# Turning the residual unscaled during the second block's output product, and one factor per token for two norms

## The reference, cut to what matters

```python
# end of the first block (layer B)
    x = x + (merged * jax.nn.silu(gate)) @ w_out_b[i]          # product "out_b"
return rmsnorm(x, norm_f)                                      # first norm
# start of the second block
shift, scale, gate = jnp.split(ada_mod(c, ada_w[i], ada_b[i]), 3, axis=-1)
h = rms_norm(x, norm_g[i]) * (1.0 + scale) + shift             # second norm, modulation
u, v, z = jnp.split(h @ w_in, 3, axis=-1)                      # products "in_v", "in_uz"
...
x = x + gate * out                                             # needs the normed x again

def rmsnorm(x, g):
    inv = lax.rsqrt(jnp.mean(xf * xf, axis=-1, keepdims=True) + RMS_EPS)
    return (xf * inv).astype(x.dtype) * g
```

## Time and profile before

| what | value |
|---|---|
| median of 3 runs | 2236.38 us (2232.61 to 2237.01) |
| profiled execution, first to last instruction | 2226.7 us |
| profiled execution's own time | not recorded apart from its span |
| TensorE busy | 2117.5 us, 95% |
| VectorE busy | 1566.4 us, 70% |
| ScalarE busy | 1079.3 us, 48% |
| HBM read | 518.00 MB, 235 GB/s over the span |

### The profile page before, as it was taken

One profiled execution on the slowest core, in us unless ns is written; L12 is line 12 of the kernel. 1 busy time (PEld: TensorE's weight loads), 2 busy tenths in 40 slices (PEclk: granted clock), 3 DMA queues, 4 the chain that ended last, 5 costly groups with the idle time before them and its releaser, 6 DMA issues. The chain is left out here.

```text
span 2226.7 us, 29663 instructions
## 1 busy us (share of the span) xinstructions
PE 2117.5 (95%) x9730; PEld 1750.1 (79%) x9730; DVE 1566.4 (70%) x2498; ACT 1079.3 (48%) x1644; POOL 11.1 (0%) x24
## 2 busy tenths in 40 slices
PE   6999999998999999979699999999999979999988
PEld 5888788887887878757588888888888868778866
DVE  5676777776789797866677777777866565556654
ACT  5444455444354445433544444544444365867732
POOL 0000000000000000000000000000000000000000
PEclk9999999999999999989799999999999989999999
DMA  6776678777766656646377878777755536434333
GB/s 275 282 287 240 235 271 321 277 289 250 275 255 238 235 226 246 230 179 254 143 287 279 306 290 296 285 283 296 281 211 177 189 133 226 173 131 148 135 132 132
DMA packets 92449, 523.32 MB, mean 235 GB/s; under 512 B 10288, under 2 KB 10416, under 8 KB 46288
## 3 DMA queue, kind: packets, MB, share of 16 engines
q1 hardware_dynamic: 89936, 510.64, 62.1%
q0 software_dynamic: 1888, 7.41, 0.9%
q10 hardware_dynamic: 544, 4.19, 0.5%
HBM read 518.00 MB, written 4.19 MB: 235 GB/s over the span
## 5 line engine op out<-in xcount | busy, mean ns | idle before, releaser
L807 ACT ACTIVATE w_hi<-raw 128x1024 fp32r<-128x1024 f32 (+1 forms) x704 | 722.1, 1046 | 946.2 <-PE bank L413 527.1
L1318 DVE TENSOR_TENSOR w_lo<-raw,w_hi 128x1024 fp32r<-128x1024 f32 (+1 forms) x704 | 829.2, 1206 | 220.1 <-ACT w_hi L807 219.5
L413 PE MATMUL bank<-w_hi,xa_hi 128*128 128x512 f32 x1952 | 773.9, 396 | 8.6 <-issue 6.1
L413 PE MATMUL bank<-w_hi,xa_lo 128*128 128x512 f32 x1952 | 764.6, 392 | 0.0
L413 PE MATMUL bank<-w_lo,xa_hi 128*128 128x512 f32 x1952 | 764.5, 392 | 0.0
L413 PEld LDWEIGHTS bank<-w_hi,xa_hi 128*128 128x128 f32 x1952 | 369.5, 189 | 86.2 <-issue 8.6
L413 PEld LDWEIGHTS bank<-w_hi,xa_lo 128*128 128x128 f32 x1952 | 369.2, 189 | 78.6
L413 PEld LDWEIGHTS bank<-w_lo,xa_hi 128*128 128x128 f32 x1952 | 369.3, 189 | 74.8
L413 PE MATMUL bank<-w_hi,xb_hi 128*128 128x512 f32 (+2 forms) x864 | 336.2, 389 | 8.5 <-DVE rbuf L1455 3.6
L413 PE MATMUL bank<-w_hi,xb_lo 128*128 128x512 f32 (+2 forms) x864 | 329.5, 381 | 0.0
L413 PE MATMUL bank<-w_lo,xb_hi 128*128 128x512 f32 (+2 forms) x864 | 329.4, 381 | 0.0
(11 more groups left out here) (204 smaller groups left out, 1204.2 us busy)
## 6 DMA issues: line engine op xcount, KB each, us to landing
raw<-units SPq DMA_DIRECT2D x352, 1024.0 KB, 4.8
ada_raw<-ada_units SPq DMA_DIRECT2D x258, 512.0 KB, 5.6
rows<-ln_rows POOLq DMA_DIRECT2D x8, 512.0 KB, 4.8
res<-x SPq DMA_DIRECT2D x2, 1024.0 KB, 6.5
held<-res ACTq DMA_DIRECT2D x1, 2048.0 KB, 8.6
res<-held ACTq DMA_DIRECT2D x1, 2048.0 KB, 7.9
out<-res SPq DMA_DIRECT2D x4, 512.0 KB, 7.4
silu_row<-c_row POOLq DMA_DIRECT2D x1, 1024.0 KB, 9.1
```

What stands on the lines that cost most here:

```text
L413: last = pe.matmul(ps[t][:, 0:cols], l, r, start=c == 0 and k == 0, stop=c == CPU * units_of - 1 and k == 2)
L807: act.activation(half_of(w_hi, n0, i), half_of(raw, n0, i), ACT.Copy).then_inc(hi_done, 1)
L1318: dve.tensor_tensor(half_of(w_lo, n0, i), half_of(raw, n0, i), half_of(w_hi, n0, i), ALU.subtract)\
```

## The change

The residual is no longer scaled before it is turned.

* During `out_b` blocks 2 and 3, TensorE turns the raw sums `res` of the finished blocks (`turn_sum`, six groups after a unit each, two more after the product). ScalarE copies each turned group to `side`, scaled per channel by `mul[:, 0]`, which is now norm_f * norm_g0 * (1 + scale0) (`scaled_group`).
* The sum of squares is taken by blocks: VectorE multiplies a block of `res` by a row of sqrt(norm_f^2 + eps) (`weigh_block`), ScalarE squares and sums it (`square_weighted`), and sums the plain squares (`square_plain`), which the first norm alone needs.
* At the border only block 3 is left to weigh and square. The reciprocal root is put on a diagonal, TensorE spreads it over the partitions with one product by ones (128x256), and VectorE multiplies each turned group by it (`scale_group`). ScalarE adds the shift and rounds to `xa_hi`, VectorE makes `xa_lo` (`lo_group`).
* The plain normed `res`, which the second block's residual sum needs, is made later: block 3's plain squares after the eighth group, and two pieces of `res` after every second block of `in_v`. The row norm_f is loaded a second time for it, from the GpSimd queue, because the first copy was overwritten by its root during `in_b`.
* Row sets that moved: `TURNS`, `SMALLS`, `HI0` and semaphore counts follow.

```diff
+            def turn_sum(g):
+
+                b0 = BLOCK0["out_b"] + g // 2
+                pe.wait_ge(bank_free[b0 % 2], read_out(b0))
+                turn(TURN0["xg"] + g, tiles(res, 2 * P * g))
+
+            product("out_b", 2, xb, then=turn_sum)
+            product("out_b", 3, xb, then=lambda q: turn_sum(4 + q) if q < 2 else None)
+            for g in (6, 7):
+                turn_sum(g)
+
+            pe.wait_ge(factor_ready, 1)
+            pe.matmul(use(SMALL0["xg"])[:, 0:S], ones, small[:, 0:S], start=True, stop=True).then_inc(small_done, 1)
...
+                if q in (7, 8, 12):
+                    b = {7: 0, 8: 1, 12: 2}[q]
+                    for t in range(NT):
+                        square_weighted(b, t, block_sums[:, t, b:b + 1])
+                    square_plain(b)
+                if 8 <= q < 14:
+                    scaled_group(q - 8)
...
-            b0 = BLOCK0["out_b"] + 3
-            residual_rms(bank_free[(b0 - 1) % 2], read_out(b0 - 1), bank_free[b0 % 2], read_out(b0))
-            residual_rms(res_normed, 3, res_normed, 4)
...
+            for t in range(NT):
+                square_weighted(3, t, stat[:, 68 + t:69 + t])
+                act.wait_ge(squared, 2 * 3 + t + 1)
+                last = act.activation(stat[:, 2 + t:3 + t], stat[:, 68 + t:69 + t], ACT.Sqrt, scale=1.0 / D,
+                                      bias=stat[:, 66 + t:67 + t])
+            last.then_inc(rms_ready, 1)
+            for g in (6, 7):
+                scaled_group(g)
+
+            for g in range(8):
+                act.wait_ge(scaled, g + 1)
...
+                last.then_inc(hi_turned, 1)
+                if g in (3, 5):
+                    split_hi(UNIT0["in_v"] + 2 + (g - 3) // 2)
+            act.wait_ge(rows_split, 8)
+            square_plain(3)
...
-            for j in range(4):
-                for t in range(NT):
-                    at = slice(j * NB, (j + 1) * NB)
-                    last = dve.scalar_tensor_tensor(out=res[:, t, at], in0=res[:, t, at], scalar=stat[:, 4 + t:5 + t],
-                                                    in1=rows[:, at], op0=ALU.mult, op1=ALU.mult)
-                last.then_inc(res_normed, 1)
...
-            residual_rows(4)
+            for t in range(NT):
+                last = dve.tensor_scalar(small[:, t * P:(t + 1) * P], ident, stat[:, 4 + t:5 + t], None, ALU.mult)
+            last.then_inc(factor_ready, 1)
...
+            dve.wait_ge(small_done, kf + 1)
+            for g in range(2):
+                scale_group(g)
+            for g in range(8):
+                lo_group(g)
+                if g < 6:
+                    scale_group(g + 2)
+                if g in (3, 5):
+                    n = (g - 3) // 2
+                    split_lo(UNIT0["in_v"] + 2 + n)
+                    add_ada(8 * ADA0["in_v"] + 2 + n)
...
             def in_v(j, first):
+                if first:
+                    dve.wait_ge(rms_ready, 4)
+                    steps.did(dve.reciprocal(stat[:, 84:86], stat[:, 82:84]))
+                    steps.wait()
+                    dve.wait_ge(row_in, 32)
...
+                for t in range(NT):
+                    cols = at_(res[:, t, :], NB * j, NB)
+                    last = dve.scalar_tensor_tensor(out=cols, in0=cols, scalar=stat[:, 84 + t:85 + t], in1=at_(rows, NB * j, NB),
+                                                    op0=ALU.mult, op1=ALU.mult)
```

More of the change, by code:

```diff
@@ L623, in in_v @@
                     product("in_v", i, xa, bs=2, us=8, j=j, first_group=TURN0["xg"] if now else None,
-                            ahead=(TURN0["xg"], side) if now else None, split=lambda g: g + 1)
+                            split=lambda g: g + 1)
             peeled(pe, 4, in_v)
@@ new lines, in scaled_group @@
+            def scaled_group(g):
+                act.wait_ge(turned, TURN0["xg"] + g + 1)
+                bank = turn_bank[(TURN0["xg"] + g) % 2]
+                for cc in range(2):
+                    c = 2 * g + cc
+                    last = act.activation(side_flat[:, c * S:(c + 1) * S], bank[:, cc * S:(cc + 1) * S], ACT.Copy,
+                                          scale=mul[:, 0, c:c + 1])
+                last.then_inc(turn_free[(TURN0["xg"] + g) % 2], 1)
+            act.wait_ge(gain_ready, 1)
@@ L1075, in modulated @@
+            act.wait_ge(rows_split, 8)
+            square_plain(3)
+            for t in range(NT):
+                steps.did(act.activation(plain_sums[:, t, :], plain_sums[:, t, :], ACT.Copy, accum_out=stat[:, 80 + t:81 + t]))
+            steps.wait()
+            act.activation(stat[:, 82:84], stat[:, 80:82], ACT.Sqrt, scale=1.0 / D, bias=eps).then_inc(rms_ready, 1)
             def modulated(g0, g, k, shift, n):
@@ L1473, in _ @@
                 dve.memset(stat[:, 72 + i:73 + i], 0.0).then_inc(s, 1)
+            steps.did(dve.memset(stat[:, 86:87], EPS * EPS))
+            steps.wait()
             residual_rows(1)
@@ L1682, in add_block, with gain, weigh_block @@
                     dve.tensor_tensor(dst, dst, banks[2 * (b0 % 2) + t][:], ALU.add).then_inc(bank_free[b0 % 2], 1)
+            def gain(k, name, scale):
+                return dve.scalar_tensor_tensor(out=mul[:, k, :], in0=mod[:, MOD0[scale]:MOD0[scale] + KC], scalar=1.0,
+                                                in1=v(name, 0, KC), op0=ALU.add, op1=ALU.mult)
+            def weigh_block(b):
+                b0 = BLOCK0["out_b"] + b
+                dve.wait_ge(root_row, 2)
+                for t in range(NT):
+                    dve.wait_ge(bank_free[b0 % 2], read_out(b0) - 1 + t)
+                    if b:
+                        dve.wait_ge(squared, 2 * b - 1 + t)
+                    dve.tensor_tensor(rbuf[:, t, :], res[:, t, b * NB:(b + 1) * NB], rows[:, b * NB:(b + 1) * NB], ALU.mult)\
+                        .then_inc(weighted, 1)
             n0, m0 = UNIT0["out_b"], 8 * ADA0["out_b"] + 2
             for q in range(16):
+                if q == 2:
+                    dve.wait_ge(mod_ready, MOD0["gate0"] // 4)
+                    steps.did(gain(0, "norm_g0", "scale0"))
+                    steps.wait()
+                    dve.tensor_tensor(mul[:, 0, :], mul[:, 0, :], v("norm_f", 0, KC), ALU.mult).then_inc(gain_ready, 1)
                 if q < 6:
@@ L1716, in _ @@
                     add_block("out_b", b)
+                    weigh_block(b)
                 if q == 13:
@@ new lines, in scale_group, with lo_group @@
+            def scale_group(g):
+                tg = TURN0["xg"] + g
+                dve.wait_ge(turn_free[tg % 2], tg // 2 + 2)
+                if g >= 4:
+                    dve.wait_ge(rows_split, g - 3)
+                dve.tensor_tensor(row_group(g).rearrange("p (k s) -> p k s", k=2),
+                                  side_flat[:, 2 * g * S:2 * (g + 1) * S].rearrange("p (k s) -> p k s", k=2),
+                                  factor, ALU.mult).then_inc(scaled, 1)
+            def lo_group(g):
+                dve.wait_ge(hi_turned, HI0["xg"] + g + 1)
+                for cc in range(2):
+                    c = 2 * g + cc
+                    last = dve.scalar_tensor_tensor(out=chunk(xa, 1, c), in0=row_group(g)[:, cc * S:(cc + 1) * S],
+                                                    scalar=mod[:, MOD0["shift0"] + c:MOD0["shift0"] + c + 1],
+                                                    in1=chunk(xa, 0, c), op0=ALU.add, op1=ALU.subtract)
+                    if g == 7 and cc == 0:
+                        last.then_inc(small_free[kf % 2], 1)
+                last.then_inc(rows_split, 1)
```

96 lines of the change are left out of this document (59 added, 37 removed).

## The result

| what | before | after |
|---|---|---|
| median of 6 runs each, same chip | 2234.96 us (2232.39 to 2237.01) | 2227.11 us (2221.49 to 2228.31) |
| ratio, 95% interval | | 0.9969 (0.9954 to 0.9984) |
| the profiled execution's span | 2226.7 us | 2226.1 us, own time 2228.05 |
| TensorE busy in it | 2117.5 us | 2122.8 us |
| end of `out_b` to start of `in_v` | 22.45 us | 10.89 us |

The change gained 7.8 us of 2235; the interval allows 3.6 to 10.3. Yet the two profiled spans differ by 0.6 us only. Both facts are true, and the experiments were needed to see why.

A forecast was written before the change was run, and what follows sets the result against it. TensorE, busy 95% of the span, was taken as the bound, with the weights' supply about as fast. Terms -11.7, +2.6 and -0.9 give -10.0; with +3.0, -7.0 us: 2229.4 us, range 2224.4 to 2234.0.

The forecast's parts named there:

- The border, 22.45 to 10.8: Between the end of `out_b` and the start of `in_v`: 22.45 us shrinks to 10.8, -11.7 us.
- the step behind it: At the border, after the product by ones: first group scaled, `xa_hi` and `xa_lo` made, `in_v` able to start at 1066.75.
- Six turns, +2.6: Six groups turned inside `out_b`, where TensorE has no idle time, cost 0.44 us each, +2.6 us.
- ScalarE as the bound of `out_b`: Rival: twelve squares and six copies in `out_b`; if none were hidden, the whole is +7.9 us, 2244.3; chance 0.06.
- Block 0, -0.9: First block of `in_v`, up to unit 4: 25.97 us becomes 25.1, -0.9 us.
- the low clock: At the start of `in_v`, TensorE at half speed for 4.3 us, costing 2.0 us, open from 0 to 3.3.
- group 6: In block 0 of `in_v`: TensorE wants this group at 1085.1, `lo_group` ends it at 1085.5, 0.4 us late.
- the wait at unit 4: In `in_v` after block 0: the unit's first half is ready 0.95 us after TensorE wants it.
- Supply in `in_v`, +3.0: Rest of `in_v`: smaller lead and VectorE's 1.35 us after every second block delay the weights, +3.0 us, between 0 and 6.9.
- 9.7 above the span, which the change doesn't touch.: Whole kernel: the median 2236.38 us lies 9.7 above the profiled span of 2226.7, and this difference stays.
- That the supply keeps up whole (-8.5 to -11): Rival: in `in_v` weights keep pace and the border's gain arrives whole, -8.5 to -11 us, about 2226.4; chance 0.24.
- That the supply eats up everything: Rival: weights set the pace in `in_v` and `in_uz`, leaving about -1 us, 2235.3, within 0.2%; chance 0.20.

The follow-up runs named there:

- c_after: The changed kernel, unchanged, timed and profiled once more against the kernel before: 2225.33 us, ratio 0.9966.
- c_before: The kernel before, unchanged, timed and profiled once more: 2231.19 us, ratio 0.9984.
- e_no_norm: The changed kernel without the eight pieces that norm `res` during `in_v`: 2223.87 us, ratio 0.9947 to the kernel before.
- e_swap: The changed kernel with VectorE making `w_lo` before the modulation's multiply-add in `in_a`, `kv`, `in_v` and `in_uz`: 2212.11 us, ratio 0.9900 to the kernel before.
- e_ada_first: The changed kernel with SyncE issuing the modulation's load ahead of the unit's weights, VectorE's order kept: 2214.18 us, ratio 0.9922 to the kernel before.
- e_swap_before: The kernel before with VectorE making `w_lo` ahead of the modulation's multiply-add: 2220.17 us, ratio 0.9937 to the kernel before.
- e_pieces: The changed kernel with three more products on VectorE ahead of each of the eight norm pieces: 2239.68 us, ratio 1.0045 to the kernel before.
- e_swap_pieces: The changed kernel with `w_lo` first and three more products ahead of each norm piece: 2220.64 us, ratio 0.9954 to the kernel before.

## Why the prediction was right, point by point

The time came out near the forecast (2227.11 against 2229.4, a gain of 7.8 us against 7.0) and the border did what the layout said. How near the total came is partly luck: the interval of 3.6 to 10.3 us would have fitted a supply term anywhere between 0 and +6.

* **The border, 22.45 to 10.8.** Measured 10.89. From the end of `out_b`: adds done after 3.5 us, roots 2.6 later, the diagonals 0.7 after that, each within 0.1 us of the layout. The 3.5 us are not the adds alone: the second half of unit 1 is still split there (ScalarE from 1058.25, `w_lo` until 1060.56), and the adds follow it. The product by ones took 1.3 where I took 0.9, inside its bounds; the step behind it 2.7 instead of 2.85.
* **Six turns, +2.6.** Blocks 2 and 3 of `out_b` took 43.68 to 43.69 us in the four profiles with the turns outside and 46.55 to 46.61 in the ten with them: +2.9, 0.48 a group instead of 0.44. No wait in them, so ScalarE as the bound of `out_b` is out: its busy time rose to 30.9 of 46.1 us and stayed hidden.
* **Block 0, -0.9.** From the first matmul of `in_v` to the first of unit 4: 25.76 before, 24.71 after, -1.0. (The 25.97 of the prediction end at ScalarE's release, 0.2 later.) The total was right, its parts less so: the low clock lasted 5.25 us, not 4.3 (2.5 us lost instead of 2.0), group 6 was not late at all, and the wait at unit 4 was 0.2, not 0.95. One profile could not give the length of the low clock: it was 5.25 us in one profile of the changed kernel and 2.70 in the other.
* **Supply in `in_v`, +3.0.** The number came near and the reason did not hold. From unit 4 to the end of `in_v` the two pairs of profiles differ by 3.2 us (155.9 against 152.7) and 4.2 us (c_after 156.5, c_before 152.3). But I took the waits of the earlier trace rows for a supply that just keeps up, and charged VectorE's added 1.35 us every second block against it. Without these pieces the waits stayed (e_no_norm, 156.7); with the modulation's data taken out of the way of `w_lo` they went (e_swap 152.3, e_ada_first). And I charged nothing to `in_uz` and `out_g`, where the first pair differs by 6.8 us and the second by 1.4. In the two profiles of the changed kernel TensorE waited 11.4 and 8.8 us for `w_lo` over the whole execution, in the two of before 5.8 and 7.7: 1 to 6 us more; by medians the loss is about 1. In the 150 us where I forecast some 3 us of waiting, 1.9 us of idle time show. One profile of each kernel can't size this term.
* **"9.7 above the span, which the change doesn't touch."** This failed. The span is 1.9 us under the time; the other 7.8 were one quick execution. It did no harm, as I added the difference to the median and not to that span. It hid what mattered: that by medians the kernel before loses about 12 us to the ring, which the profile of a quick execution shows less of.
* **Rivals.** That the supply keeps up whole (-8.5 to -11) is what the kernels with `w_lo` first come close to: 8.1 us by medians. Their profiled spans differ by 11.1 us: +2.8 up to the end of `out_b`, -11.55 in the border, -1.3 in the stretch and -1.0 behind `out_g`. The 3 us between 11.1 and 8.1 are the choice of executions: the profiled one of e_swap is 0.85 us under its median, that of e_swap_before the slowest of its six, 2.2 over. That the supply eats up everything is what one pair of single executions looks like, and what the medians rule out.

## What to carry to other kernels

Where an engine waits for transfers all the time and the next transfer is issued only when it has finished, follow one buffer round its ring, from issue to issue, and compare that time with what the consumer needs; a wait of 0.5 us in one execution says little about the next. An instruction on a shared engine that waits for a transfer of its own must not stand ahead of the one on which the bound engine hangs, or its transfer must be issued first. And turned round everywhere, the same rule can harm: behind the last unit of `out_b` the multiply-add was in the way of what comes next, by 1.2 us.

## What I had not expected of the hardware

After TensorE had waited 3.49 us for a `w_lo` in e_pieces, the matmuls behind it ran at 0.43 us each, the granted clock being 0.50; windows of that kernel:

```profile
1141.00:1142.00 1.00, 1.00 (x3) 0.79 (x3) 0.35 (x1) 0.00 (x0) 0.00 (x0) 0.50 0.98 418
1142.00:1143.00 1.00, 1.00 (x5) 0.76 (x4) 0.00 (x0) 0.00 (x0) 0.00 (x0) 0.78 0.92 377
```

From 1136.8 to 1142.1 it ran at the lower of its two levels, 1.2 GHz, which costs another 2.5 us. Behind waits of 1.11 us (e_swap_pieces) and 1.66 us (the changed kernel) the matmuls kept 0.23 us; behind the one of 3.02 us in e_swap_pieces five of them kept it, and then they took 0.43 each until 1263.8. So in these runs one long wait was dearer than the same time in short ones. At the start of `in_v` the low clock lasted 5.25 us in one execution of the changed kernel and 2.7 us in the other, from the same program.
